# Two of the four weight sums of each seven-product group on GpSimd instead of VectorE

## The chip, the cores and the metric
One core of a Trainium2 chip runs the kernel; the other seven are not used. The metric is the device time of one execution in microseconds (us), the median of three runs.

## The reference
One decoder layer on x of 256 tokens by 2048 channels, all float32. Every stage starts with an RMSNorm:
```python
x = x + 0.5 * swiglu(rmsnorm(x, ffn1_norm), w_gate, w_up, w_down)     # 2048 -> 5632 -> 2048
h = rmsnorm(x, mix_norm)
proj = h @ w_in                                                       # q, k, v of two mixers, gates
y_dil, y_fox = dilated_attention(...), forgetting_attention(...)      # 8 heads of 128 each
merged = sigmoid(g_d + b) * (y_dil @ w_proj_dil) + sigmoid(g_f + b) * (y_fox @ w_proj_fox)
x = x + merged @ w_out
x = x + 0.5 * swiglu(rmsnorm(x, ffn2_norm), w_gate2, w_up2, w_down2)
return rmsnorm(x, final_norm)
def swiglu(x, w_gate, w_up, w_down): return (silu(x @ w_gate) * (x @ w_up)) @ w_down
```
The change touches only the two feed-forward stages (`swiglu`).

## The kernel before
**Precision.** Every float32 weight `w` is used as two parts of the rounded type: ScalarE copies it into `w_hi`, VectorE computes `w_lo = w - w_hi`, and the same is done for activations. A product is three matmuls (hi hi, hi lo, lo hi), so each weight passes through ScalarE and VectorE once before TensorE may use it.

**Slabs and the ring.** The unit is a slab, two 128-row blocks of 512 columns (128 partitions x 1024 elements). SyncE loads weights in pieces of two slabs (1 MB) into the four buffers `raw`. In the feed-forward stages the split slabs live in a ring of six (`FFN_RING`): `w_hi`/`w_lo` for four of them, `more_hi`/`more_lo` for two. ScalarE may round slab n when TensorE has finished slab n - 6 (semaphore `slab_done`), VectorE splits it after that (`hi_ready`), TensorE waits for the split (`lo_ready`), and SyncE reuses a buffer of `raw` by the count of `lo_ready` in the table `FREE` (lines 84, 424): loads 4 and 5 of a step, the gate and up rows of group 1, go out when the slabs before 5 and before 7 are split; loads 0 and 1 of the coming step when those before -6 and before -4 are.

**A feed-forward step.** The hidden width of 5632 is worked through in eleven chunks of 512. The first is done plainly (`FIRST`, 16 slabs), the ten others are the steps of a loop (`STEPS`, 30 slabs each), and there are two such stages, `ffn(0)` and `ffn(1)`, with the mixers between them: 20 steps in all. A step has, in this order (`step_slab`, line 88): seven slabs of group 0, four plain slabs 7 to 10, seven slabs 11 to 17 of group 1, four plain slabs 18 to 21, and eight slabs 22 to 29 of the down projection for the chunk before. A plain or down slab takes 12 matmuls, a group's slab 6.

**A group** computes gate and up for both token halves from seven products instead of eight, in the manner of Strassen and Winograd. Four of the seven weight operands are sums of blocks of the raw gate weights G and up weights U (even and odd rows of blocks):
```python
PRODUCTS = (("sum", T3), ("sum", T1), ("gate", 1), ("sum", T4), ("gate", 0), ("sum", T2), ("up", 1))
# T3 = U[odd] - U[even]   T1 = U[even] - G[even]   T2 = T3 + G[even]   T4 = G[odd] - T2
```
They lie in `sums`, one set of four 128x1024 tiles for both groups, and count as slabs 0, 1, 3 and 5 of their group. ScalarE rounds them like any slab (`round_step`, line 912, waiting on `summed`), VectorE splits them (`split_step`, line 1191).

**The order of the work** is written out by hand on each engine, each queue is in order, and semaphores alone join the queues. ScalarE and VectorE run six slabs ahead of TensorE in their programs: in the loop's slot o they handle slab o + 6. On VectorE, `early_sums` (line 1181) makes T3 and T1 of group 1 just before the split of slab 10, and those of the next step's group 0 just before the split of slab 29; it first waits for the load. T2 follows the split of the group's first slab and T4 that of its second.

**The hidden chunk.** TensorE transposes the chunk's hidden activations (line 585), the two token halves one after the other in one PSUM bank; ScalarE rounds each half into `hT_hi` (line 959) and VectorE makes `hT_lo` (line 1263). The second half's rounding stands behind the rounding of slab 11 in ScalarE's program (slot o == 5), and its `hT_lo` behind the split of slab 11 and T2 in VectorE's. TensorE waits for it between slabs 8 and 9 (line 657); slab 9 begins with line 694 (`direct_up`). Lines 520 to 522 are the matmuls of plain slabs, 533 to 535 those of a group, 1283 the add of a down result to `xres`.

**GpSimd** has no program in this kernel.

Of the kernel before, what the change touches and what calls it, by code (L numbers as in the profile page):

```python
# [80 lines left out]
PRODUCTS = (("sum", T3), ("sum", T1), ("gate", 1), ("sum", T4), ("gate", 0), ("sum", T2), ("up", 1))  # L81
SUMS = 8 * STEPS

# [88 lines left out]
def build(nc, x, ffn1_norm, ffn1_w_gate, ffn1_w_up, ffn1_w_down, mix_norm, w_in, b_forget,  # L172
# [144 lines left out]
    final_gain_landed = sem("final_gain_landed")  # L317
    stored = sem("stored")
    summed = sem("summed")
    s_ready = sem("s_ready")  # L320
# [74 lines left out]
    block = nc.Block()  # L395
    with block:

        @block.sync
# [494 lines left out]
        def _(act):  # L893
# [18 lines left out]
            def round_step(place, offset, count):  # L912

                q, r = divmod(offset, STEP)
                kind, g, o = step_slab(r)
                src, l = step_source(r)
                if l is None:
                    act.wait_ge(summed, count + 8 * q + 4 * g + (T3, T1, T2, T4).index(PRODUCTS[o][1]) + 1)
                else:
                    act.wait_ge(raw_landed[l % LOADS], place.landed(STEP_LOADS * q + l))  # L920
                act.wait_ge(slab_done, place.slab(offset - FFN_RING + 1))
                nc.scalar.activation(slot_hi(place, offset), src, ACT.Copy).then_inc(hi_ready, 1)  # L922
# [70 lines left out]
            def ffn(f, b):  # L993
# [26 lines left out]
                def step(place, i, last):  # L1020
                    merged = (i + f * STEPS) * COMBINED
                    for o in range(STEP):
                        if not last or o + FFN_RING < STEP:
                            round_step(place, o + FFN_RING, i * 8 + count)
                        else:
# [141 lines left out]
        def _(dve):  # L1167
# [12 lines left out]

            def early_sums(place, q, g):

                gate, up = 0, 1
                dve.wait_ge(raw_landed[up], place.landed(STEP_LOADS * q + 4 * g + up))
                nc.vector.tensor_tensor(sums[:, T3], raw[:, up, 1::2, :], raw[:, up, 0::2, :],
                                        ALU.subtract).then_inc(summed, 1)
                dve.wait_ge(raw_landed[gate], place.landed(STEP_LOADS * q + 4 * g + gate))
                nc.vector.tensor_tensor(sums[:, T1], raw[:, up, 0::2, :], raw[:, gate, 0::2, :],
                                        ALU.subtract).then_inc(summed, 1)

            def split_step(place, offset, count, final=False):

                q, r = divmod(offset, STEP)
                if r in (10, STEP - 1) and not (final and r == STEP - 1):

                    early_sums(place, *((q, 1) if r == 10 else (q + 1, 0)))
                kind, g, o = step_slab(r)
# [3 lines left out]
                if kind == "paired" and o in (0, 1):  # L1201
                    done, gate = count + 8 * q + 4 * g, 0
                    if o == 0:
                        dve.wait_ge(summed, done + 1)
                        nc.vector.tensor_tensor(sums[:, T2], sums[:, T3], raw[:, gate, 0::2, :],
                                                ALU.add).then_inc(summed, 1)
                    else:
                        dve.wait_ge(summed, done + 3)
                        nc.vector.tensor_tensor(sums[:, T4], raw[:, gate, 1::2, :], sums[:, T2],  # L1209
# [106 lines left out]
            def ffn(f, b):  # L1316
                first = first_place(f)
                silu, count = f * FF_CHUNKS * TT, f * SUMS
                for o in range(FIRST):
                    m = o + FFN_RING  # L1320
                    if m < FIRST:
                        if m == FIRST - 1:
                            early_sums(step_place(f), 0, 0)
                        split_slab(first, m)
# [31 lines left out]
                def step(place, i, last):  # L1356
                    hid, merged = i * TT + HID[f], (i + f * STEPS) * COMBINED
                    u3, u2 = partial[:, PART_U3], partial[:, PART_U2]
                    for o in range(STEP):
                        if not last or o + FFN_RING < STEP:  # L1360
                            split_step(place, o + FFN_RING, i * 8 + count, last)
                        else:
# [224 lines left out]
```

## Time and profile before
| what | value |
|---|---|
| median of three runs | 2142.38 us (2140.95 to 2144.67) |
| the profiled execution | 2140.0 us, its span 2138.2 us |
| granted TensorE clock, mean | 0.996 of full |
| busy: TensorE, VectorE, ScalarE, GpSimd | 98%, 75%, 51%, 0% |
| DMA | 402.88 MB, 188 GB/s |

The times of the engines overlap: a share of busy time says how full an engine is, and not what it costs. A VectorE record of 1.22 us is followed by the next 1.14 us later, so the records of a stream overlap a little; the matmul records of 0.39 us follow one another every 0.23 us. "Idle before" names what ended an engine's idle time. PE is TensorE, DVE is VectorE, ACT is ScalarE, POOL is GpSimd, SP is SyncE.

### The profile page before, as it was taken

Reading aid. Unit: us, or ns where it says so; the run is one execution under the profiler, and the core shown is the slowest. Engines: PE = TensorE matmul, PEld = TensorE weight load, DVE = VectorE, ACT = ScalarE, POOL = GpSimd, SP = SyncE. Lnnn points to the kernel's source line nnn. Section 1 sums busy time; section 2 is a strip of 40 time slices with the busy share of each in tenths; the row PEclk is TensorE's granted clock in tenths of the full one; section 3 lists DMA queues with packets and bytes.
Section 4 is the critical chain, followed back from the end, with each engine's and each line's share of the span. In section 5 each row is a group of like instructions: output and inputs, shape, how many; then the busy total and the mean of one; then the engine's idle time right before and its main releaser. Section 6 shows DMA issues by size and latency. Waiting matters only on the chain.

```text
span 2138.2 us, 26519 instructions
## 1 busy us (share of the span) xinstructions
PE 2097.6 (98%) x9475; PEld 1728.2 (81%) x9475; DVE 1606.8 (75%) x1613; ACT 1090.8 (51%) x1259; POOL 0.2 (0%) x4
## 2 busy tenths in 40 slices
PE   7999999999999999999999999999999999999997
PEld 5788888888887888888888888878888888888876
DVE  6888888888888744444455555688888889888886
ACT  5545555545555544555454344465555555555553
POOL 0000000000000000000000000000000000000000
PEclk9999999999999999999999999999999999999999
DMA  7556566556566545545445665555565665555652
GB/s 247 187 167 215 177 217 214 182 171 216 177 216 207 167 158 180 188 160 171 158 164 183 204 206 185 189 190 199 162 204 188 216 206 195 166 201 188 220 198 98
DMA packets 204643, 402.88 MB, mean 188 GB/s; under 512 B 8576, under 2 KB 8752, under 8 KB 204464
## 3 DMA queue, kind: packets, MB, share of 16 engines
q1 hardware_dynamic: 202032, 401.64, 56.1%
q10 hardware_dynamic: 2560, 0.55, 0.1%
q8 instruction: 34, 0.56, 0.1%
q14 instruction: 17, 0.14, 0.0%
HBM read 400.06 MB, written 2.10 MB: 188 GB/s over the span
## 4 chain that ended last, share of the span: by engine, by line
PE 93%; DVE 3%; ACT 2%; DMA 1%; issue 1%; SPq 0%; ACTq 0%; DVEq 0%
PE ps L520 21%; PE ps L522 21%; PE ps L521 21%; PE ps L533 6%; PE ps L535 6%; PE ps L534 6%; PE ps L694 3%; PE ps L696 3%; PE ps L695 3%; PE ps L585 1%; DMA raw<-in_ffn_w_gate 1%; DMA raw<-in_ffn_w_up 1%; DVE xres L1283 1%; DVE w_lo L1178 1%; ACT chunk_buf L946 0%
## 5 line engine op out<-in xcount | busy, mean ns | idle before, releaser
L1178 DVE TENSOR_TENSOR w_lo<-raw,w_hi 128x1024 fp32r<-128x1024 f32 x256 | 312.6, 1224 | 312.2 <-ACT w_hi L909 311.9
L909 ACT ACTIVATE w_hi<-raw 128x1024 fp32r<-128x1024 f32 x256 | 269.8, 1059 | 313.0 <-PE ps L522 307.1
L922 ACT ACTIVATE w_hi<-raw 128x1024 fp32r<-128x1024 f32 x300 | 317.8, 1059 | 218.0 <-PE ps L522 97.6
L1199 DVE TENSOR_TENSOR w_lo<-raw,w_hi 128x1024 fp32r<-128x1024 f32 x300 | 366.4, 1221 | 77.3 <-ACT w_hi L922 66.5
L520 PE MATMUL ps<-w_hi,xT_hi 128*128 128x512 f32 x816 | 321.6, 394 | 7.1 <-DVE w_lo L1178 6.7
L522 PE MATMUL ps<-w_hi,xT_lo 128*128 128x512 f32 x816 | 318.6, 390 | 0.0
L521 PE MATMUL ps<-w_lo,xT_hi 128*128 128x512 f32 x816 | 318.3, 390 | 0.0
L520 PE MATMUL ps<-w_hi,hT_hi 128*128 128x512 f32 x576 | 224.4, 390 | 0.0
L522 PE MATMUL ps<-w_hi,hT_lo 128*128 128x512 f32 x576 | 224.1, 389 | 0.0
L521 PE MATMUL ps<-w_lo,hT_hi 128*128 128x512 f32 x576 | 224.1, 389 | 0.0
L922 ACT ACTIVATE w_hi<-sums 128x1024 fp32r<-128x1024 f32 x100 | 106.2, 1062 | 223.0 <-DVE sums L1209 111.8
L922 ACT ACTIVATE more_hi<-raw 128x1024 fp32r<-128x1024 f32 x140 | 148.6, 1062 | 103.0 <-PE ps L522 70.8
L1199 DVE TENSOR_TENSOR more_lo<-raw,more_hi 128x1024 fp32r<-128x1024 f32 x140 | 169.4, 1221 | 39.7 <-ACT more_hi L922 34.3
L520 PEld LDWEIGHTS ps<-w_hi,xT_hi 128*128 128x128 f32 x816 | 153.8, 189 | 38.7 <-issue 7.2
L522 PEld LDWEIGHTS ps<-w_hi,xT_lo 128*128 128x128 f32 x816 | 153.6, 188 | 32.5
L521 PEld LDWEIGHTS ps<-w_lo,xT_hi 128*128 128x128 f32 x816 | 153.9, 189 | 30.7
L1199 DVE TENSOR_TENSOR w_lo<-sums,w_hi 128x1024 fp32r<-128x1024 f32 x100 | 122.2, 1222 | 37.6 <-ACT w_hi L922 36.3
L1283 DVE SCALAR_TENSOR_TENSOR xres<-ps,xres 128x1024 f32<-128x1024 f32 x104 | 126.4, 1216 | 6.2 <-PE ps L522 6.2
L694 PE MATMUL ps<-w_hi,xT_hi 128*128 128x512 f32 x320 | 125.2, 391 | 1.9 <-DVE hT_lo L1263 1.9
L522 PEld LDWEIGHTS ps<-w_hi,hT_lo 128*128 128x128 f32 x576 | 108.1, 188 | 22.5
L521 PEld LDWEIGHTS ps<-w_lo,hT_hi 128*128 128x128 f32 x576 | 108.2, 188 | 22.4
L520 PEld LDWEIGHTS ps<-w_hi,hT_hi 128*128 128x128 f32 x576 | 108.1, 188 | 22.3
(212 smaller groups left out, 3635.6 us busy)
## 6 DMA issues: line engine op xcount, KB each, us to landing
raw<-in_ffn_w_gate SPq DMA_DIRECT2D x88, 1024.0 KB, 5.1
raw<-in_ffn_w_up SPq DMA_DIRECT2D x88, 1024.0 KB, 5.2
raw<-in_ffn_w_down SPq DMA_DIRECT2D x88, 1024.0 KB, 5.1
raw<-in_w_in SPq DMA_DIRECT2D x80, 1024.0 KB, 5.0
raw<-in_w_out SPq DMA_DIRECT2D x16, 1024.0 KB, 5.0
raw<-in_w_proj_dil SPq DMA_DIRECT2D x8, 1024.0 KB, 5.0
raw<-in_w_proj_fox SPq DMA_DIRECT2D x8, 1024.0 KB, 4.9
xres<-in_x SPq DMA_DIRECT2D x4, 512.0 KB, 7.1
```

The lines of the kernel that those rows point to most:

```text
L520: nc.tensor.matmul(acc, hi, hi_w[:, j], start=first and j == 0, stop=False)
L521: nc.tensor.matmul(acc, hi, lo_w[:, j], start=False, stop=False)
L522: done = nc.tensor.matmul(acc, lo, hi_w[:, j], start=False, stop=last and j == 1)
L533: nc.tensor.matmul(acc, hi, hi_w[:, j], start=first and j == 0, stop=False)
L534: nc.tensor.matmul(acc, hi, lo_w[:, j], start=False, stop=False)
L535: done = nc.tensor.matmul(acc, lo, hi_w[:, j], start=False, stop=last and j == 1)
L694: nc.tensor.matmul(acc, hi, hi_w[:, j], start=begin, stop=False)
L909: nc.scalar.activation(slot_hi(place, offset), raw_half(place, offset), ACT.Copy).then_inc(hi_ready, 1)
L922: nc.scalar.activation(slot_hi(place, offset), src, ACT.Copy).then_inc(hi_ready, 1)
L1178: nc.vector.tensor_tensor(slot_lo(place, offset), raw_half(place, offset), slot_hi(place, offset).bitcast(F32), ALU.subtract).then_inc(lo_ ...
L1199: nc.vector.tensor_tensor(slot_lo(place, offset), step_source(r)[0], slot_hi(place, offset).bitcast(F32), ALU.subtract).then_inc(lo_ready, 1)
L1283: nc.vector.scalar_tensor_tensor(xres[:, :, chunk(n)], ps[:, banks:banks + TT], factor, xres[:, :, chunk(n)], ALU.mult, ALU.add)\
```

## The change
T3 and T1 are made by a program of GpSimd's own: for both feed-forward stages a loop over the ten steps, in it both groups. It waits until the slabs before slab -6 (group 0) or before slab 6 (group 1) are split, then for the up load, makes T3, waits for the gate load, makes T1. These two count on a new semaphore `early_summed`; T2 and T4 stay on VectorE and count on `summed`, and their waits and ScalarE's are counted anew. The semaphores' order and the data are the same otherwise.
```diff
--- before.py
+++ after.py
@@ -79,7 +79,7 @@
 PAIR_SLABS = 7
 
 PRODUCTS = (("sum", T3), ("sum", T1), ("gate", 1), ("sum", T4), ("gate", 0), ("sum", T2), ("up", 1))
-SUMS = 8 * STEPS
+SUMS = 4 * STEPS
 
 FREE = (-6, -4, -2, 0, 5, 7, 9, 11, 16, 18, 20, 22)
 GROUP_ORDER = (1, 0, 3, 2)
@@ -316,6 +316,7 @@
     gate_bias_landed = sem("gate_bias_landed")
     final_gain_landed = sem("final_gain_landed")
     stored = sem("stored")
+    early_summed = sem("early_summed")
     summed = sem("summed")
     s_ready = sem("s_ready")
     s_hi = sem("s_hi")
@@ -395,6 +396,24 @@
     block = nc.Block()
     with block:
 
+        @block.gpsimd
+        def _(pool):
+            gate, up = 0, 1
+            for f in range(2):
+                with pool.Fori(0, STEPS) as i:
+                    place = step_place(f, i)
+                    for g in range(2):
+                        if g == 0:
+                            pool.wait_ge(lo_ready, place.slab(-6))
+                        else:
+                            pool.wait_ge(lo_ready, place.slab(6))
+                        pool.wait_ge(raw_landed[up], place.landed(4 * g + up))
+                        nc.gpsimd.tensor_tensor(sums[:, T3], raw[:, up, 1::2, :], raw[:, up, 0::2, :],
+                                                ALU.subtract).then_inc(early_summed, 1)
+                        pool.wait_ge(raw_landed[gate], place.landed(4 * g + gate))
+                        nc.gpsimd.tensor_tensor(sums[:, T1], raw[:, up, 0::2, :], raw[:, gate, 0::2, :],
+                                                ALU.subtract).then_inc(early_summed, 1)
+
         @block.sync
         def _(sp):
             sp.dma_start(gain_rows[0:KT, :], ffn1_norm.rearrange("l (k p) -> (l k) p", p=P))\
@@ -915,7 +934,8 @@
                 kind, g, o = step_slab(r)
                 src, l = step_source(r)
                 if l is None:
-                    act.wait_ge(summed, count + 8 * q + 4 * g + (T3, T1, T2, T4).index(PRODUCTS[o][1]) + 1)
+                    made = early_summed if PRODUCTS[o][1] in (T3, T1) else summed
+                    act.wait_ge(made, count + 4 * q + 2 * g + (T3, T1, T2, T4).index(PRODUCTS[o][1]) % 2 + 1)
                 else:
                     act.wait_ge(raw_landed[l % LOADS], place.landed(STEP_LOADS * q + l))
                 act.wait_ge(slab_done, place.slab(offset - FFN_RING + 1))
@@ -1021,7 +1041,7 @@
                     merged = (i + f * STEPS) * COMBINED
                     for o in range(STEP):
                         if not last or o + FFN_RING < STEP:
-                            round_step(place, o + FFN_RING, i * 8 + count)
+                            round_step(place, o + FFN_RING, i * 4 + count)
                         else:
                             round_slab(last_place(f), o + FFN_RING - STEP)
                         if o == 2:
@@ -1178,34 +1198,21 @@
                 nc.vector.tensor_tensor(slot_lo(place, offset), raw_half(place, offset),
                                         slot_hi(place, offset).bitcast(F32), ALU.subtract).then_inc(lo_ready, 1)
 
-            def early_sums(place, q, g):
-
-                gate, up = 0, 1
-                dve.wait_ge(raw_landed[up], place.landed(STEP_LOADS * q + 4 * g + up))
-                nc.vector.tensor_tensor(sums[:, T3], raw[:, up, 1::2, :], raw[:, up, 0::2, :],
-                                        ALU.subtract).then_inc(summed, 1)
-                dve.wait_ge(raw_landed[gate], place.landed(STEP_LOADS * q + 4 * g + gate))
-                nc.vector.tensor_tensor(sums[:, T1], raw[:, up, 0::2, :], raw[:, gate, 0::2, :],
-                                        ALU.subtract).then_inc(summed, 1)
-
             def split_step(place, offset, count, final=False):
 
                 q, r = divmod(offset, STEP)
-                if r in (10, STEP - 1) and not (final and r == STEP - 1):
-
-                    early_sums(place, *((q, 1) if r == 10 else (q + 1, 0)))
                 kind, g, o = step_slab(r)
                 dve.wait_ge(hi_ready, place.slab(offset + 1))
                 nc.vector.tensor_tensor(slot_lo(place, offset), step_source(r)[0],
                                         slot_hi(place, offset).bitcast(F32), ALU.subtract).then_inc(lo_ready, 1)
                 if kind == "paired" and o in (0, 1):
-                    done, gate = count + 8 * q + 4 * g, 0
+                    done, gate = count + 4 * q + 2 * g, 0
                     if o == 0:
-                        dve.wait_ge(summed, done + 1)
+                        dve.wait_ge(early_summed, done + 1)
                         nc.vector.tensor_tensor(sums[:, T2], sums[:, T3], raw[:, gate, 0::2, :],
                                                 ALU.add).then_inc(summed, 1)
                     else:
-                        dve.wait_ge(summed, done + 3)
+                        dve.wait_ge(summed, done + 1)
                         nc.vector.tensor_tensor(sums[:, T4], raw[:, gate, 1::2, :], sums[:, T2],
                                                 ALU.subtract).then_inc(summed, 1)
 
@@ -1319,8 +1326,6 @@
                 for o in range(FIRST):
                     m = o + FFN_RING
                     if m < FIRST:
-                        if m == FIRST - 1:
-                            early_sums(step_place(f), 0, 0)
                         split_slab(first, m)
                     else:
                         split_step(step_place(f), m - FIRST, count)
@@ -1358,7 +1363,7 @@
                     u3, u2 = partial[:, PART_U3], partial[:, PART_U2]
                     for o in range(STEP):
                         if not last or o + FFN_RING < STEP:
-                            split_step(place, o + FFN_RING, i * 8 + count, last)
+                            split_step(place, o + FFN_RING, i * 4 + count, last)
                         else:
                             split_slab(last_place(f), o + FFN_RING - STEP)
                         if o == 2:
```

## Rows read from the trace of the kernel before
**Rows 1.** The page, part 1: busy us, share of the span, instructions, by engine.
```profile
PE 2097.6 (98%) x9475; PEld 1728.2 (81%) x9475; DVE 1606.8 (75%) x1613; ACT 1090.8 (51%) x1259; POOL 0.2 (0%) x4
```

**Rows 2.** Waits of TensorE: engine and line, released by; us in total, times, longest.
```profile
PE ps L520 <- DVE w_lo L1178: 6.7, 2, 4.1
...
PE ps L694 <- DVE hT_lo L1263: 1.9, 2, 1.1
```

**Rows 3.** VectorE timeline, third step: start us, us, line, operation, tiles, idle before.
```profile
208.94 1.21 DVE L1199 TENSOR_TENSOR w_lo<-raw,w_hi 128x1024 fp32r<-128x1024 f32 x1
210.74 1.23 DVE L1185 TENSOR_TENSOR sums<-raw 128x1024 f32<-128x1024 f32 x1 [0.59 <-DMA raw<-in_ffn_w_up]
211.89 1.22 DVE L1188 TENSOR_TENSOR sums<-raw 128x1024 f32<-128x1024 f32 x1
213.02 1.22 DVE L1199 TENSOR_TENSOR w_lo<-raw,w_hi 128x1024 fp32r<-128x1024 f32 x1
214.16 1.22 DVE L1199 TENSOR_TENSOR w_lo<-sums,w_hi 128x1024 fp32r<-128x1024 f32 x1
215.29 1.22 DVE L1205 TENSOR_TENSOR sums<-sums,raw 128x1024 f32<-128x1024 f32 x1
216.43 0.68 DVE L1263 TENSOR_TENSOR hT_lo<-ps,hT_hi 128x512 fp32r<-128x512 f32 x1
```

**Rows 4.** Timeline of TensorE in the same step.
```profile
217.05 0.39 PE L522 MATMUL ps<-w_hi,xT_lo 128*128 128x512 f32 x1
217.27 0.47 PE L694 MATMUL ps<-w_hi,xT_hi 128*128 128x512 f32 x1
```

**Rows 5.** Timelines, VectorE and TensorE: first step, last of `ffn(0)`.
```profile
86.91 0.68 DVE L1263 TENSOR_TENSOR hT_lo<-ps,hT_hi 128x512 fp32r<-128x512 f32 x1
...
88.78 0.39 PE L694 MATMUL ps<-w_hi,xT_hi 128*128 128x512 f32 x1
...
667.82 0.68 DVE L1263 TENSOR_TENSOR hT_lo<-ps,hT_hi 128x512 fp32r<-128x512 f32 x1
...
668.56 0.50 PE L694 MATMUL ps<-w_hi,xT_hi 128*128 128x512 f32 x1 [1.15 <-DVE hT_lo L1263]
```

**Rows 6.** Timeline of VectorE where the third and the fourth step begin.
```profile
204.21 2.35 DVE L1199 TENSOR_TENSOR more_lo<-raw,more_hi 128x1024 fp32r<-128x1024 f32 x2
...
266.27 1.22 DVE L1199 TENSOR_TENSOR w_lo<-sums,w_hi 128x1024 fp32r<-128x1024 f32 x1 [0.38 <-ACT w_hi L922]
```

**Rows 7.** Waits of VectorE.
```profile
DVE sums L1185 <- DMA raw<-in_ffn_w_up: 12.1, 19, 2.0
```

**Rows 8.** Groups of VectorE instructions: count, busy us, mean ns, idle before.
```profile
L1185 DVE TENSOR_TENSOR sums<-raw 128x1024 f32<-128x1024 f32 x40 | 48.8, 1220 | 12.1 <-DMA raw<-in_ffn_w_up 12.1
L1188 DVE TENSOR_TENSOR sums<-raw 128x1024 f32<-128x1024 f32 x40 | 48.7, 1218 | 0.0
```

**Rows 9.** Timeline of VectorE, end of the third step.
```profile
251.06 1.22 DVE L1185 TENSOR_TENSOR sums<-raw 128x1024 f32<-128x1024 f32 x1
...
255.60 1.21 DVE L1199 TENSOR_TENSOR more_lo<-sums,more_hi 128x1024 fp32r<-128x1024 f32 x1
```

**Rows 10.** Timeline of ScalarE, third step.
```profile
208.82 1.06 ACT L922 ACTIVATE w_hi<-raw 128x1024 fp32r<-128x1024 f32 x1 [0.23 <-PE ps L535]
...
212.08 1.06 ACT L922 ACTIVATE w_hi<-sums 128x1024 fp32r<-128x1024 f32 x1 [2.20 <-DVE sums L1185]
...
213.05 0.57 ACT L959 ACTIVATE hT_hi<-ps 128x512 fp32r<-128x512 f32 x1
```

**Rows 11.** Timeline of SyncE: when loads are issued.
```profile
214.27 0.37 SPq L425 DMA_DIRECT2D raw<-in_ffn_w_up  x1
...
240.32 0.37 SPq L425 DMA_DIRECT2D raw<-in_ffn_w_up  x1
```

**Rows 12.** The page, part 6: DMA issues, KB each, median us to landing.
```profile
raw<-in_ffn_w_up SPq DMA_DIRECT2D x88, 1024.0 KB, 5.2
```

**Rows 13.** Busy time in one step's stretch, by engine (instructions), TensorE clock, DMA share.
```profile
201.00:265.30 64.30, 64.11 (x284) 52.47 (x284) 56.38 (x52) 34.04 (x36) 0.00 (x0) 1.00 0.58 196
```

## The prediction
> **What bounds the kernel now.** I read the page first, then the waits of TensorE, then one feed-forward step instruction by instruction. TensorE is busy for 98% of the span and VectorE for 75%, while GpSimd does nothing [rows 1]. So time can only be won where TensorE stands idle, and is lost wherever it is made to. Its waits are few: 6.7 us for splits of the plain stages, and 1.9 us, in two of the twenty steps, in front of line 694 [rows 2]. None of its waits in the feed-forward steps is for `sums` or for a slab made from them. By throughput the four sums of a group cost VectorE nothing that TensorE feels.
>
> By latency it is another matter. TensorE may not begin slab 9 of a step (line 694) before the second half of `hT_lo` is written (line 657). Follow VectorE in one step [rows 3]: it splits slab 9, stands idle until the `up` load of group 1 lands, at T = 210.74, and then does in program order T3, T1, the split of slab 10, the split of slab 11 (whose rounding needs T3), T2, and only then `hT_lo`, which starts at 216.43 and takes 0.68: written at 217.11, 6.37 us after T. TensorE streams without a gap and starts line 694 at 217.27 [rows 4]. The slack is 0.16 us. I read the same pair in all 20 steps: it is 1.19 us in the first (87.59 to 88.78), 0.13 to 0.40 in seventeen others, and in the last step of each feed-forward TensorE waits, 1.15 and 0.72 us [rows 5]. The twenty slacks add up to 5.9 us; the hand-over from `hT_lo` to line 694 takes 0.06 (668.50 to 668.56), which leaves about 4.7 us to use up in all.
>
> T itself does not move with the change. The `up` load is issued when slab 6 is split (204.21 plus 1.14), and that split comes behind slab 5's and an add to `xres`; where the next step begins, the split of slab 5 starts at 266.27 after 0.38 us of waiting for ScalarE [rows 6], so VectorE has by then worked off its backlog, and the pace is TensorE's. VectorE waits for this load in 19 of 20 steps, 12.1 us in sum [rows 7].
>
> **The change, part by part.**
> *Removed from VectorE:* 40 T3 and 40 T1, 1.22 us each in the records, 1.14 from start to start [rows 3, 8]: 80 x 1.14 = 91 us. Half are done at the step's end, where VectorE is behind (the T3 at 251.06 and the T1 after it) and has caught up by 266.27 [rows 6, 9]; TensorE does not wait there, so 46 us are worth nothing. The other half stand in the chain T to `hT_lo`, where 2.28 us per step leave.
>
> *Added to the chain:* the same two sums on GpSimd, and two hand-overs. No record of before shows a GpSimd sum. From below its price is VectorE's, 1.14 us; from above three passes over 1024 elements, two operands in and one out, one after the other, at ScalarE's 1.06 us for a one-operand pass [rows 10], 3.2 us. I take two such passes (an engine that fetches its operands in turn and writes beside that), 2.12, and 0.11 for the hand-over from T3's end to the rounding (211.97 to 212.08) [rows 3, 10]: P = 2.23 us. By the Trainium skill, GPSIMD Engine Reference, Reconciling with measured numbers, 2048 float32 elements take GpSimd 4497 ns and VectorE 2293; half of the former is 2.25 us, by which the sum below would be about 1 us larger. This trace shows VectorE's 1.22 for 1024 and no GpSimd sum.
>
> *Whether the two engines stand in each other's way* is the second unknown. From below nothing; from above each waits for a whole instruction of the other, since all of VectorE's splits, like GpSimd's sums, read two operands from SBUF. I take the upper end. In the chain that has two places:
> - Split 10 no longer queues behind the sums. Its rounding ends at 209.88 [rows 10] and split 9 at 210.08, so it runs 210.08 to 211.22, over the landing: T3 starts at T + 0.5.
> - T1 follows T3 at once on GpSimd, as the `gate` half has landed long before. The rounding of slab 11 takes 1.06 after T3, less than P, so split 11 always finds T1 running and waits for its end: T + 0.5 + 2P.
>
> Then split 11, T2 and `hT_lo` follow as before, 2.95 us (214.16 to 217.11) [rows 3]. Sum: T + 0.5 + 4.46 + 2.95 = T + 7.91 against T + 6.37, **1.54 us late per step**. Twenty steps give 31 us, less the 4.7 us of slack: +26 us. Nothing is hidden here, because line 694 is next on TensorE's in-order queue; what is late next, the split of slab 12 and T4, is not needed before TensorE has done slabs 9 and 10 (5.4 us) and slab 11.
>
> The rule behind this choice is in the Trainium skill, SBUF — State Buffer, Who interferes with whom: a VectorE instruction with two SBUF inputs and a GpSimd instruction that reads SBUF share a read interface, and the later one blocks fully until the other ends. Nothing in this trace can show it. By it the sum is the +26 above, without it the first rival's.
>
> *GpSimd at the step's end (group 0):* T3 and T1 can run from the landing of load 1 (issued at 240.32, 5.2 us to landing: near 245.5) [rows 11, 12] to about 250. At worst they hold up one or two splits by up to 2.2 us each, while VectorE saves 2.28 us and still finishes slab 0's split some 10 us before TensorE needs it (split at 255.60, used from 265.3 on) [rows 9, 13]. Cost nothing; if that cover were gone, up to 2 us per step.
> *Waits and queues:* GpSimd's new waits stall nobody else, its queue holds only these sums. Its wait for slab 6 (group 1) is over before the `up` load is even issued. SyncE's loads: the one that waits for split 10 is issued some 3 us earlier (at 214.27 now) [rows 11], and nobody waited for it. VectorE's own wait for T3 before T2 is over when split 11 is done. ScalarE's rounding of slab 11 now hangs on GpSimd, with the second `hT_hi` behind it (0.57 us) [rows 10], inside the time above. The sums in slot order are otherwise the same data, no DMA is added, and two loops on GpSimd run beside all else.
>
> The profiled execution took 2140.0 us (span 2138.2) and the median of the runs is 2142.4; 2142.4 + 26 = **2168 us**. A measurement of this kernel can tell about 0.2%, 4.3 us, from no change.
>
> **The rivals.**
> *No interference.* Then T3 starts at T, and the chain is P + 1.06 for the rounding + 0.1 + 2.95 = T + 6.34, as late as before. T1 runs beside the split. TensorE feels nothing, at best the two waits of 1.9 us shrink: 2140 to 2144 us. For it: the chain has two sums less on VectorE, and 98% of TensorE leaves no more to win. Against it: it needs P under about 2.5 us too (6.37 + 0.29 slack). Above that point every further 0.1 us costs 2 us. 17%.
> *A GpSimd sum near the upper end, 2.8 to 3.2 us.* With interference the lateness is 0.5 + 6.4 + 2.95 - 6.37 = 3.5 us per step, 70 - 5 = +65: 2207 us; at 2.8, +49, 2191. Without it, about 1.0 per step, +15: 2158. 17%.
> *A sum near VectorE's own price, 1.14 to 1.5 us.* With interference 0.5 + 2.28 + 2.95 is T + 5.7, earlier than now: the two waits vanish, 2140.5 us; decisive is P under 1.7. I know no reason for such a pace. 3%.
> *The change doesn't do what it says:* GpSimd's loop is held up by its waits or by its own loop instructions, so that T3 comes 1 us or more after the landing even without interference. Each 1 us costs 20 us: 2158 to 2170. The waits above speak against it; 3%.
>
> **How the numbers follow.** The forecast has a chance of 60%, with P between 1.9 and 2.6: lateness 0.9 to 2.3 us per step, 2155 to 2184 on its own. The range goes down to the first rival's and up into the second's: 2140 to 2192; outside are the upper part of the long sums and little else. Faster by over 0.2% would need 4.3 us, more than the two waits hold: 2%. Within 0.2%: 17 + 3 and the few forecasts that all but fit the slack, less the 2: 20%. Slower: 78%.
>
> **What the changed profile would show.** If right: 80 GpSimd sums, about 2.2 us each; TensorE waiting for `hT_lo` in front of line 694 in 18 or more steps, some 1.3 us each and about 28 us in sum; VectorE's split 11 starting only when T1 ends (or its record longer by that wait), and T3 starting after split 10 rather than at the landing; every step about 65.6 us where it is 64.3 [rows 13]. VectorE's busy time falls by some 97 us, unless waiting counts as busy. Wrong if: split 11 starts 0.1 us after its rounding while T1 runs (no interference), sums of another length, or TensorE waiting for a slab (`w_lo`) at lines 520 or 533 instead, which would put the damage in the ring.

## The result and the profile after

The changed kernel took 2170.35 us (median of 4 runs, 2169.03 to 2172.27) against 2142.64 us before (4 runs of the same session): ratio 1.013, 95% interval 1.0112 to 1.0147. It is 27.7 us slower; the forecast was 2168, a loss of 26.

The page of the changed kernel, parts 1 and 5 (groups: line, engine, operation, tiles, count, then busy us and mean ns, then idle before); line 713 is what line 694 was [rows 1, 8]:

```profile
PE 2097.3 (97%) x9475; PEld 1729.4 (80%) x9475; DVE 1567.2 (72%) x1533; ACT 1091.0 (50%) x1259; POOL 221.9 (10%) x84
...
L411 POOL TENSOR_TENSOR sums<-raw 128x1024 f32<-128x1024 f32 x40 | 107.3, 2684 | 1860.4 <-DMA raw<-in_ffn_w_up 1860.4
L1206 DVE TENSOR_TENSOR w_lo<-sums,w_hi 128x1024 fp32r<-128x1024 f32 x100 | 142.9, 1429 | 120.2 <-ACT w_hi L942 118.9
...
L713 PE MATMUL ps<-w_hi,xT_hi 128*128 128x512 f32 x320 | 126.9, 396 | 28.0 <-DVE hT_lo L1270 28.0
```

TensorE does the same work (2097 us) in a span of 2168.9 instead of 2138.2 us, so all of the loss is idle time. GpSimd is now busy for 222 us: in the records its sums take 2.68 us (T3) and 2.90 us (T1) on the mean. VectorE lost 80 instructions of 1.22 us, 98 us, but its busy time fell by 40 only, from 1606.8 to 1567.2; the splits of `sums`, 1.22 us on the mean before, read 1.43. So waiting does count as busy in these records, the case that the prediction left open.

The waits of TensorE in the changed kernel (us in total, times, longest); the second line of [rows 2] answers to the first:

```profile
PE ps L713 <- DVE hT_lo L1270: 28.0, 20, 1.4
PE ps L552 <- DVE xres L1290: 7.4, 16, 0.5
```

1.9 us in two steps have become 28.0 us in all twenty, 1.4 us each. The 7.4 us for `xres` in front of line 552, the third product of a step, are new as well, and need a second look (below: they cost nothing).

GpSimd in the changed kernel's third step, group 1 and then group 0 of the next step:

```profile
212.59 2.79 POOL L411 TENSOR_TENSOR sums<-raw 128x1024 f32<-128x1024 f32 x1 [23.73 <-DMA raw<-in_ffn_w_up]
215.34 2.40 POOL L414 TENSOR_TENSOR sums<-raw 128x1024 f32<-128x1024 f32 x1
249.08 2.40 POOL L411 TENSOR_TENSOR sums<-raw 128x1024 f32<-128x1024 f32 x1 [31.34 <-DMA raw<-in_ffn_w_up]
251.44 3.39 POOL L414 TENSOR_TENSOR sums<-raw 128x1024 f32<-128x1024 f32 x1
```

VectorE in the same step, for [rows 3]:

```profile
210.79 2.35 DVE L1206 TENSOR_TENSOR w_lo<-raw,w_hi 128x1024 fp32r<-128x1024 f32 x2
216.59 2.24 DVE L1206 TENSOR_TENSOR w_lo<-sums,w_hi 128x1024 fp32r<-128x1024 f32 x1 [3.45 <-ACT w_hi L942]
218.75 1.21 DVE L1212 TENSOR_TENSOR sums<-sums,raw 128x1024 f32<-128x1024 f32 x1
219.89 0.68 DVE L1270 TENSOR_TENSOR hT_lo<-ps,hT_hi 128x512 fp32r<-128x512 f32 x1
```

Read the two together. The first VectorE row is two splits, slabs 9 and 10, and ends at 213.14. The load has landed at 212.59, where GpSimd's T3 begins in the record; it lasts 2.79 us, where an undisturbed sum lasts 2.40 (the rows at 215.34 and 249.08), so it really ran from 212.98, when the split of slab 10 was all but through. T1 follows at 215.34 and ends at 217.74. The split of slab 11 is due at 216.59 and lasts 2.24 us instead of 1.22: it began in truth at 217.6, at the end of T1. T2 and `hT_lo` follow as they did, `hT_lo` is written at 220.57, and line 713 starts at 220.69 [rows 4]. The other steps confirm the reading: T3's record starts 5.99 to 6.44 us after the step's third product, as the load lands, but ends 9.11 to 9.17 us after it in all twenty.

A table of three stretches, from TensorE's starts, shows where in a step the time lies (mean us per step; A: third product to slab 9, B: slab 9 to slab 20, where the second `direct_up` pair begins, both over twenty steps; C: slab 20 to the next step's third product, over the eighteen steps that another one follows):

| kernel | A | B | C | sum |
|---|---|---|---|---|
| before | 13.07 | 20.45 | 30.98 | 64.50 |
| changed | 14.43 | 20.53 | 30.98 | 65.94 |
| e1_group0 | 12.86 | 20.41 | 30.98 | 64.25 |
| e2_group1 | 14.56 | 20.67 | 30.98 | 66.21 |
| e3_t1_late | 13.46 | 20.53 | 31.22 | 65.21 |
| e4_no_meeting | 13.10 | 20.47 | 31.24 | 64.81 |
| e5_before_swap | 12.98 | 20.42 | 30.75 | 64.15 |
| e6_group0_swap | 12.93 | 20.41 | 30.28 | 63.62 |
| e7_after_swap | 14.48 | 20.53 | 30.28 | 65.29 |
| e8_spare_read | 14.81 | 21.18 | 30.98 | 66.97 |
| e9_spare_write | 13.00 | 20.44 | 30.98 | 64.42 |
| e10_earlier_sums | 12.86 | 20.41 | 30.28 | 63.55 |

Twenty times 1.36 (A) and 0.08 (B) are 29 of the 30.7 us by which the span grew.

Three steps of the kernel before are not like the others. In the last step of each stage the `up` load landed 7.7 and 7.3 us after the third product instead of 6.2. In its very first, A is 14.48 instead of 12.88, because TensorE had a lower granted clock there (us; busy and instructions of TensorE, its loads, VectorE, ScalarE, GpSimd; granted clock; DMA share, GB/s):

```profile
74.30:78.00 3.70, 3.70 (x9) 2.99 (x10) 2.04 (x2) 0.74 (x1) 0.00 (x0) 0.54 0.40 92
```

The profiles of e3, e4, e5 and e6 have the same stretch in that step; the changed kernel's and the others do not. Differences in A of less than 0.1 us between kernels say nothing for that reason. In the seventeen ordinary steps A grew by 1.56 and B by 0.09 us.

Times and ratios below are medians against runs of the kernel before on the same chip, there 2138.9 to 2140.7 us.

### The profile page after: what moved, and what is told of

It is laid out like the page before. It is cut to its first block, busy times and chain, and to the rows that moved or that the text cites. A ratio compares the mean times of both kernels' runs of the same rounds, so it can differ in the third digit from the quotient of the medians.

```text
span 2168.9 us, 26517 instructions
## 1 busy us (share of the span) xinstructions
PE 2097.3 (97%) x9475; PEld 1729.4 (80%) x9475; DVE 1567.2 (72%) x1533; ACT 1091.0 (50%) x1259; POOL 221.9 (10%) x84
## 4 chain that ended last, share of the span: by engine, by line
PE 78%; issue 10%; DVE 5%; ACT 3%; POOL 3%; DMA 1%; SPq 0%; ACTq 0%; DVEq 0%; POOLq 0%
PE ps L539 19%; PE ps L541 19%; PE ps L540 19%; PE ps L713 4%; PE ps L715 3%; PE ps L714 3%; PE ps L554 3%; PE ps L553 3%; PE ps L552 3%; POOL sums L411 3%; ACT w_hi L942 2%; DVE w_lo L1206 1%; DVE sums L1212 1%; DMA raw<-in_ffn_w_gate 1%; DVE hT_lo L1270 1%
## 5 line engine op out<-in xcount | busy, mean ns | idle before, releaser
L1198 DVE TENSOR_TENSOR w_lo<-raw,w_hi 128x1024 fp32r<-128x1024 f32 x256 | 316.9, 1242 | 313.0 <-ACT w_hi L928 312.7
L1206 DVE TENSOR_TENSOR w_lo<-raw,w_hi 128x1024 fp32r<-128x1024 f32 x300 | 376.1, 1259 | 75.3 <-ACT w_hi L942 64.5
L411 POOL TENSOR_TENSOR sums<-raw 128x1024 f32<-128x1024 f32 x40 | 107.3, 2684 | 1860.4 <-DMA raw<-in_ffn_w_up 1860.4
L1206 DVE TENSOR_TENSOR w_lo<-sums,w_hi 128x1024 fp32r<-128x1024 f32 x100 | 142.9, 1429 | 120.2 <-ACT w_hi L942 118.9
```

The lines of the kernel that those rows point to most:

```text
L411: nc.gpsimd.tensor_tensor(sums[:, T3], raw[:, up, 1::2, :], raw[:, up, 0::2, :], ALU.subtract).then_inc(early_summed, 1)
L1198: nc.vector.tensor_tensor(slot_lo(place, offset), raw_half(place, offset), slot_hi(place, offset).bitcast(F32), ALU.subtract).then_inc(lo_ ...
L1206: nc.vector.tensor_tensor(slot_lo(place, offset), step_source(r)[0], slot_hi(place, offset).bitcast(F32), ALU.subtract).then_inc(lo_ready, 1)
```

## The experiments

### Which group does the harm: e1_group0 and e2_group1
GpSimd's loop keeps one group; `early_sums` comes back on VectorE for the other, at its old place. The diff is e1_group0's; e2_group1 has `(1,)`, and the call for group 0 before the split of slab 29 as in the kernel before.
```diff
-                    for g in range(2):
+                    for g in (0,):
...
+                if r == 10:
+                    early_sums(place, q, 1)
```


> Only group 0's T3 and T1 on GpSimd, group 1's back on VectorE at its old place. Theory A (the damage is group 1's chain from the landing of the up load to hT_lo, through the length of the sums and the two engines waiting for each other): the chain is the one of before, 6.37 us after the landing, so the wait for hT_lo falls back to about 2 us in sum and the time to 2140 to 2145 us, although two VectorE records at each step's end stay longer. Rival B (any GpSimd sum slows the kernel, by blocking VectorE wherever it runs): half the sums, half the loss, about 2156 us.

Measured 2136.97 us, ratio 0.999 (0.9981 to 1.000); before took 2139.25 on this chip, so the time lies below the range expected and the ratio does not.

> Only group 1's T3 and T1 on GpSimd, group 0's back on VectorE. Theory A: all of the loss stays, 2168 to 2172 us, with 28 us of waiting for hT_lo. The wait of 7.4 us for xres at the head of the step, new in the changed kernel, goes, and the gap of 0.2 us without a named releaser in front of slab 0 comes back, with no change in the time, since the third product starts 30.98 us after the second plain group in both. Rival B: about 2156 us.

Measured 2175.75 us, ratio 1.0162 (1.0146 to 1.0179), above the changed kernel's 1.013. Waits of TensorE in e2_group1:

```profile
PE ps L713 <- DVE hT_lo L1283: 30.8, 20, 3.3
...
PE ps L552 <- issue: 4.4, 18, 0.3
```

All of the loss is group 1's. In e1_group0 the two GpSimd sums of a step take 2.5 and 3.3 us in the records, and VectorE's records next to them are longer, yet A, B and C are those of before or less: rival B fell. It won 2 us (the interval reaches 1.000), as much as the two waits for `hT_lo` in the last steps, which are gone; the rest of its lower A is the first step. e2_group1 lies 4 us above what was expected in three of its four runs (2175.8 us; the fourth took 2170.96), and its profiled execution has it in one place, the first step of the second stage (A 16.30, B 23.18, where nearly all its other steps have 14.4 and 20.5). There the `up` load took 7.6 us to land instead of 5.1, TensorE waited 3.3 us for `hT_lo`, and its granted clock was 0.50 over the 3.7 us behind the wait. Why the load was late is not shown. As expected, the wait for `xres` is gone and the gap is back, at the same C.

### Take the meetings away: e3_t1_late and e4_no_meeting
```diff
                         pool.wait_ge(raw_landed[gate], place.landed(4 * g + gate))
+                        if g == 1:
+                            pool.wait_ge(ht_lo, i * TT + (HID[f] + TT))
```
e4_no_meeting has this too, and in `split_step`:
```diff
+                if r == 10:
+                    dve.wait_ge(early_summed, count + 4 * q + 3)
```


> The changed kernel, in which GpSimd starts group 1's T1 only when the second half of hT_lo is written. Theory A: T1 no longer stands in the way of the split of slab 11 (1.0 us per step), so hT_lo comes at the landing + 0.4 + 2.4 + 1.2 + 2.95 = 6.95 us, 0.3 to 0.6 us late: line 713 waits 0.4 us instead of 1.4 in each step and the time is 2148 to 2153 us, faster although a wait is added. T1 of slab 12 comes 3.7 us later but is hidden under slabs 9 and 10. Rival C (the engines do not wait for each other; the whole loss is that a GpSimd sum takes 2.4 to 2.8 us instead of 1.2): the time stays at 2170 us or rises.

Measured 2155.48 us, ratio 1.0076 (1.0059 to 1.0093): above the 2148 to 2153 expected.

> As e3_t1_late, and VectorE splits slab 10 only after T3 of group 1 is made, so that neither of the two sums of group 1 meets a VectorE instruction. Theory A: T3's record falls from 2.8 to 2.4 us and starts at the landing; the split of slab 10 runs beside ScalarE's rounding of slab 11. hT_lo at the landing + 2.4 + 1.2 + 2.95 = 6.55 us, within the slack of 0.3 us: 2141 to 2147 us, so the mere length of the sums costs next to nothing. Rival C: still 15 us or more above before.

Measured 2143.26 us, ratio 1.0018 (1.0008 to 1.0027). GpSimd in e4_no_meeting, then VectorE:

```profile
210.62 2.39 POOL L411 TENSOR_TENSOR sums<-raw 128x1024 f32<-128x1024 f32 x1 [23.46 <-DMA raw<-in_ffn_w_up]
217.30 2.39 POOL L416 TENSOR_TENSOR sums<-raw 128x1024 f32<-128x1024 f32 x1 [4.30 <-DVE hT_lo L1274]
```
```profile
208.88 1.22 DVE L1210 TENSOR_TENSOR w_lo<-raw,w_hi 128x1024 fp32r<-128x1024 f32 x1
213.13 1.23 DVE L1210 TENSOR_TENSOR w_lo<-raw,w_hi 128x1024 fp32r<-128x1024 f32 x1 [3.03 <-POOL sums L411]
214.27 1.22 DVE L1210 TENSOR_TENSOR w_lo<-sums,w_hi 128x1024 fp32r<-128x1024 f32 x1
215.41 1.22 DVE L1216 TENSOR_TENSOR sums<-sums,raw 128x1024 f32<-128x1024 f32 x1
216.54 0.68 DVE L1274 TENSOR_TENSOR hT_lo<-ps,hT_hi 128x512 fp32r<-128x512 f32 x1
```

Two added waits take the ratio from 1.013 to 1.0018, 24 us. T3 lasts 2.39 us from the landing on; the split of slab 10 waits for it and is done beside ScalarE's rounding; the split of slab 11 lasts 1.22 us. `hT_lo` is written at 217.22, 6.60 us after the landing, and A is 13.10, as before. So sums of twice the length leave the chain 0.2 us longer than before and all but fit the slack, and rival C, that the length alone did it, fell. By A, T1 against the split of slab 11 cost 0.97 us per step (e3), T3 against the split of slab 10 0.36 (e4); in ordinary steps, without the first and those around the stages' ends, it is 1.02 and 0.55.

That a later T1 would be hidden was wrong for both. C grew by 0.25 us per step. In e3_t1_late the down loads go out later and closer together, group 0's `up` load lands 6.75 us after its issue (242.09 to 248.84) where it took 5.3 (243.77 to 249.08 in the changed kernel), and GpSimd's group 0 T3 (248.84 to 251.25) then starts just ahead of the split of slab 28 and holds it up for nearly its whole length. VectorE, then TensorE:

```profile
249.00 3.33 DVE L1208 TENSOR_TENSOR w_lo<-raw,w_hi 128x1024 fp32r<-128x1024 f32 x1 [1.49 <-ACT w_hi L944]
...
265.94 1.21 DVE L1292 SCALAR_TENSOR_TENSOR xres<-ps,xres 128x1024 f32<-128x1024 f32 x1
```
```profile
267.76 0.49 PE L554 MATMUL ps<-more_hi,pair_hi 128*128 128x512 f32 x1 [0.85 <-DVE xres L1292]
```

The first row is that split, 3.33 us instead of 1.22; the second is the third add to `xres`, which is late by it, and for which TensorE then waits in front of the next step's slab 0. It waits for an add to `xres` for 9.7 us in 13 steps, in nine of them for this third one, in the others for the fourth. This is the remainder to before in e4 as well (10.4 us in 14 steps).

### The dispute by itself: e8_spare_read and e9_spare_write
The kernel before, with a GpSimd loop whose result nobody uses (what it writes, `gate_buf`, is free in these steps; ScalarE waits for `spare_done` before it uses it).
```diff
+                with pool.Fori(0, STEPS - 1) as i:
+                    place = step_place(f, i)
+                    pool.wait_ge(spare_done, i * 1 + (1 + f * (STEPS - 1) * 1))
+                    pool.wait_ge(raw_landed[up], place.landed(4 + up))
+                    nc.gpsimd.tensor_tensor(gate_buf[:, 0]..., xT_hi[:, 0:4].bitcast(F32),
+                                            xT_lo[:, 0:4].bitcast(F32), ALU.subtract)
```
e9_spare_write subtracts one column instead and then does a `memset` of `gate_buf`, 2047 columns.

> The kernel before, all four sums on VectorE, and beside it one GpSimd subtraction of the same size per step (18 of the 20 steps), started at the landing of group 1's up load, that reads parts of xT_hi and xT_lo and writes a buffer nobody reads. No instruction of the layer waits for it in those steps. Theory A (a GpSimd instruction that reads SBUF and a VectorE instruction with two SBUF inputs exclude each other): one VectorE record in the chain grows by up to 2.4 us, hT_lo comes 0.3 to 2.1 us late, and the time is 5 to 38 us above before, most likely about 2160 to 2175 us. Rival C (only the length of the sums mattered): no VectorE record grows and the time is that of before.

Measured 2191.59 us, ratio 1.0251 (1.0227 to 1.0275). Timelines of e8_spare_read, GpSimd and VectorE:

```profile
213.44 3.45 POOL L408 TENSOR_TENSOR gate_buf<-xT_hi,xT_lo 128x1024 f32<-128x1024 f32 x1 [63.03 <-DMA raw<-in_ffn_w_up]
```
```profile
213.40 1.22 DVE L1201 TENSOR_TENSOR sums<-raw 128x1024 f32<-128x1024 f32 x1 [0.52 <-DMA raw<-in_ffn_w_up]
214.54 3.43 DVE L1204 TENSOR_TENSOR sums<-raw 128x1024 f32<-128x1024 f32 x1
217.89 1.22 DVE L1215 TENSOR_TENSOR w_lo<-raw,w_hi 128x1024 fp32r<-128x1024 f32 x1
```

This is the cleanest picture of the mechanism. VectorE's T3 starts first, at 213.40, and keeps its 1.22 us. GpSimd's instruction, released at 213.44, lasts 3.45: about 1.05 of waiting and 2.40 of work, until 216.89. VectorE's T1, due at 214.54, lasts 3.43: it stands still until GpSimd is done. No instruction of these steps depends on GpSimd's result, and the kernel is 51 us slower. More than was expected: 35 us are in A, and 15 us in B, by a second effect that the last section shows.

> As e8_spare_read, but GpSimd subtracts one column only and then fills 2047 columns with a constant, so that it is busy for 1 to 3 us at the same place and reads next to nothing. Theory A with the shared read side alone: no VectorE record grows by more than 0.1 us and the time is within 3 us of before. Rival F (any GpSimd instruction that touches SBUF blocks VectorE): as e8_spare_read.

Measured 2140.58 us, ratio 1.000 (0.9991 to 1.001). Timelines of e9_spare_write, GpSimd and VectorE:

```profile
209.19 1.23 POOL L408 TENSOR_TENSOR gate_buf<-xT_hi,xT_lo 128x1 f32<-128x1 f32 x1 [61.29 <-DMA raw<-in_ffn_w_up]
210.35 1.81 POOL L410 MEMSET gate_buf<- 128x2047 f32 x1
```
```profile
209.14 1.23 DVE L1202 TENSOR_TENSOR sums<-raw 128x1024 f32<-128x1024 f32 x1 [0.46 <-DMA raw<-in_ffn_w_up]
210.28 1.22 DVE L1205 TENSOR_TENSOR sums<-raw 128x1024 f32<-128x1024 f32 x1
211.42 1.22 DVE L1216 TENSOR_TENSOR w_lo<-raw,w_hi 128x1024 fp32r<-128x1024 f32 x1
```

GpSimd is busy from 209.19 to 212.16, and its `memset`, 1.81 us of that, lies across two VectorE instructions, T1 and the split behind it, that keep their 1.22 us. So a GpSimd instruction that only writes SBUF excludes nothing here, and rival F fell; that the `memset` is also another kind of instruction than a subtraction is not separated by this run. The trace agrees with the rule of the Trainium skill, SBUF — State Buffer, Who interferes with whom, by which a VectorE instruction with two SBUF inputs contends with a GpSimd instruction that reads SBUF and not with one that only writes it.

### The head of the step: e5_before_swap, e6_group0_swap, e7_after_swap, e10_earlier_sums
Why did the new wait of 7.4 us for `xres` cost nothing, C being 30.98 in both kernels? TensorE at the fourth step's head, before:

```profile
264.75 0.39 PE L522 MATMUL ps<-w_hi,hT_lo 128*128 128x512 f32 x1
265.36 0.49 PE L533 MATMUL ps<-more_hi,pair_hi 128*128 128x512 f32 x1 [0.22 <-issue]
...
268.76 0.49 PE L533 MATMUL ps<-w_hi,xT_hi 128*128 128x512 f32 x1
```

and in the changed kernel:

```profile
268.20 0.39 PE L541 MATMUL ps<-w_hi,hT_lo 128*128 128x512 f32 x1
268.42 0.39 PE L552 MATMUL ps<-more_hi,pair_hi 128*128 128x512 f32 x1
...
272.20 0.49 PE L552 MATMUL ps<-w_hi,xT_hi 128*128 128x512 f32 x1 [0.46 <-DVE xres L1290]
```

Before, slab 0 starts 0.61 us after the last matmul of the step, where the pace is 0.23; after, it starts at the pace, and the third product waits for `xres` instead. From the last matmul to the third product it is 4.01 and 4.00 us. In the program there are two candidates: the loop ends with a wait for the third add to `xres`, which VectorE in its backlog has only then, and the third product waits for the fourth add, which stands behind the split of slab 5. VectorE before:

```profile
263.54 1.21 DVE L1283 SCALAR_TENSOR_TENSOR xres<-ps,xres 128x1024 f32<-128x1024 f32 x1
...
267.41 1.22 DVE L1283 SCALAR_TENSOR_TENSOR xres<-ps,xres 128x1024 f32<-128x1024 f32 x1
```

The third add ends at 264.75, when the last matmul starts, and the fourth at 268.63, 0.13 before the third product. The edit, called the swap below, puts that add ahead of the split:
```diff
                     for o in range(STEP):
+                        if o == STEP - 1:
+                            add_down(place, STEP, NN - 1, DOWN_BANKS[NN - 1], 0.5)
                         if not last or o + FFN_RING < STEP:
...
-                        if o > STEP - DOWN and o % 2 == 1:
+                        if STEP - DOWN < o < STEP - 1 and o % 2 == 1:
```


> The kernel before, in which VectorE adds the fourth down result to xres ahead of the split of the next step's slab 5 and not behind it. Theory D (in the kernel before, two limits tie at the head of a step: VectorE's backlog, which releases the third add to xres just too late for the loop's last wait and costs the gap of 0.4 to 0.5 us in front of slab 0, and this fourth add): only one of the two is taken away, so little is won, 0 to 3 us. What may shrink is the chain to hT_lo, since the split of slab 6 comes 0.4 us earlier: 2137 to 2140 us if before stands at 2139. Rival E (the gap in front of slab 0 is the loop's own cost and nothing is tied to it): the same 0 to 3 us, so this run speaks only together with e6_group0_swap.

Measured 2133.45 us, ratio 0.9967 (0.9954 to 0.9979): 7 us where 0 to 3 were expected. The gap in front of slab 0 is there still (3.5 us in 16 steps), but C fell by 0.23 us: the fourth add had been the later of the two by that much. The waits of the last steps for `hT_lo` fell from 1.9 to 0.6 us (A by 0.09).

> e1_group0 (only group 0's T3 and T1 on GpSimd) with the same swap as e5_before_swap. Theory D: GpSimd's sums take away the backlog and with it the gap in front of slab 0, the swap takes away the wait of 7.4 us for xres, and the third product can start 0.46 us earlier in each of 16 steps or more: 7 to 9 us less than e1_group0, about 2129 us. Rival E: the gap comes back in another place and the time stays at 2136 us.

Measured 2125.77 us, ratio 0.9928 (0.9911 to 0.9945). C is 30.28, 0.70 less than before, where GpSimd's group 0 sums alone gave nothing and the swap alone 0.23. That is 11 us below e1_group0, where 7 to 9 were expected, and the gap did not come back in another place: rival E fell. Two limits that tie must both go.

> The changed kernel with the swap of e5 and e6 (the fourth add to xres ahead of the split of slab 5). Theory D: the wait for xres (7.4 us) goes, and because the split of slab 6, the issue and the landing of group 1's up load move 0.4 us ahead against TensorE, the wait for hT_lo shrinks by about 0.4 us per step as well: 2170 - 7 - 8 = about 2155 us. If only the wait for xres were removed: 2163 us.

Measured 2158.55 us, ratio 1.0095 (1.0078 to 1.0112). C fell by 0.70, but A not at all. The landing moved ahead, and T3 did not: GpSimd in e7_after_swap:

```profile
210.83 3.10 POOL L411 TENSOR_TENSOR sums<-raw 128x1024 f32<-128x1024 f32 x1 [22.72 <-DMA raw<-in_ffn_w_up]
213.90 2.40 POOL L414 TENSOR_TENSOR sums<-raw 128x1024 f32<-128x1024 f32 x1
```

T3's record starts 6.0 us after the third product (204.82), where in the changed kernel it was 6.3, but ends after 9.11 us in both (213.93 here; 215.38 after 206.27). What lets T3 in is the end of the split of slab 10, which hangs on TensorE's pace, and not the landing: the expectation that A would gain 0.4 us was wrong, and this is why. T3's record ends 9.11 to 9.18 us after the third product in nineteen steps of this kernel; in the one left the load itself landed late.

e10_earlier_sums has the swap on the kernel before, no GpSimd, and
```diff
-                if r in (10, STEP - 1) and not (final and r == STEP - 1):
+                if r in (10, STEP - 2) and not (final and r == STEP - 2):
```


> The kernel before with the swap, no GpSimd: VectorE makes group 0's T3 and T1 one slab earlier (ahead of the split of slab 28 of the step before and not 29), in the 2.7 us in which it otherwise idles there. Theory D (what GpSimd's group 0 sums are worth is only that VectorE is through its backlog sooner): most of the gap in front of slab 0 goes without GpSimd, 2126 to 2131 us if before stands at 2140. Rival: only GpSimd's help removes the backlog, and the time stays at that of e5_before_swap, 0.997 of before.

Measured 2124.72 us, ratio 0.9936 (0.992 to 0.9953), the same as e6_group0_swap within the intervals. VectorE in e10_earlier_sums:

```profile
242.52 1.22 DVE L1185 TENSOR_TENSOR sums<-raw 128x1024 f32<-128x1024 f32 x1
243.65 1.22 DVE L1188 TENSOR_TENSOR sums<-raw 128x1024 f32<-128x1024 f32 x1
244.79 1.22 DVE L1199 TENSOR_TENSOR w_lo<-raw,w_hi 128x1024 fp32r<-128x1024 f32 x1
...
258.84 1.22 DVE L1283 SCALAR_TENSOR_TENSOR xres<-ps,xres 128x1024 f32<-128x1024 f32 x1
...
262.04 1.22 DVE L1283 SCALAR_TENSOR_TENSOR xres<-ps,xres 128x1024 f32<-128x1024 f32 x1 [0.40 <-PE ps L522]
```

T3 and T1 of group 0 fill a stretch in which VectorE idled, the third add is done at 260.06, 4.9 us before the third product (264.92) where it was 4.0, and the fourth waits for TensorE alone. All that GpSimd did for this kernel VectorE does by itself, with the sums one slab earlier and the swap. Against the kernel before it wins 14 us, where the changed kernel loses 28.

## Why the prediction was right

**The place** was right: the loss is the wait for `hT_lo` in front of slab 9, 28.0 us of waiting against about 28 named, in 20 steps of 1.4 us against "18 or more, some 1.3 us each", and a step takes 65.9 us against 65.6. No wait for a slab of the ring appeared, and e1 and e2 put it all in group 1.

**The chain**, term by term: T + 0.5 for the split of slab 10 was 0.4 in the third step and 0.48 on the mean of all. P, taken as 2.23 with 0.11 for a hand-over in it, was too small: a sum takes 2.40 in the record, and 2.35 from start to start where two undisturbed ones follow each other (e2_group1, first step of the second stage). `hT_lo` came 7.98 us after T in the third step (212.59 to 220.57) and 7.88 to 8.31 in all, 8.07 on the mean of the ordinary ones, against 7.91. The estimate of 2.25 us by the Trainium skill, GPSIMD Engine Reference, Reconciling with measured numbers, is the length of a sum without a hand-over. The rows' figure to set beside it is 2.12, and the measured 2.40 is above both.

**The choice** between no interference and whole-instruction exclusion, which nothing in the trace of before could decide, was the step on which all hung; e8 shows exclusion directly, e9 that a GpSimd `memset` is free of it, and e4 about what the first rival would have given: a ratio of 1.0018, which is 2146.5 us where before takes 2142.6, just above its 2140 to 2144, and the excess is in C, where the sums of group 0 still meet VectorE. The rival of a GpSimd sum near 3 us looks right in the records (2.68 and 2.90 on the mean), but they hold the waiting; the undisturbed rows say 2.40.

**Luck in the number.** The forecast loss was made of 1.3 us in each ordinary step and 3.5 us in the three others. Measured by A and B it was 1.65 us in each of seventeen ordinary steps, 28.0 us, and 0.9 in the three others. The ordinary steps lost more because `hT_lo` came 1.70 us later and not 1.54, because the hand-over to line 713 takes 0.13 us there and not 0.06, and by the 0.09 in B. The three others lost less: the slack of 1.19 us in the first step stood behind TensorE's lower clock and was not there in the changed kernel, and the last steps' late landings, which the prediction took as given, did not come again. The first error is 6 us, the second 3 us the other way, so the number came out closer than its terms.

**What was missed:** "TensorE does not wait there, so 46 us are worth nothing" held in time and not in its reason. TensorE did lose 0.70 us per step at the step's head to VectorE's backlog (C 30.98 against 30.28 in e6 and e10), 0.4 to 0.5 of it in a gap without a named releaser; that gap stayed worth nothing because the fourth add to `xres` tied with it. And a stop costs TensorE a little beyond its length: the matmul after it is followed 0.1 us late, the 0.08 us in B. Against the forecast 26 us, all of them in A, stand 27 in A and 2 in B.

## What to carry to other kernels
Moving work off a busy engine helps only if that engine's throughput is what is waited for; here it was the latency of one chain, with 0.1 to 0.4 us of slack in most steps, and what its links lose beyond that is lost in every step. GpSimd arithmetic that reads SBUF is not parallel to VectorE instructions with two SBUF operands: count both engines' instructions as one queue wherever they meet, and place GpSimd's where VectorE idles or takes one operand from PSUM. A new wait that costs nothing points at a tie: look for the older limit under it, since removing both may pay.

## What was not expected of the hardware
**A short stop can cost more than itself.** In e8_spare_read, eight of twenty steps have B at 22.1 to 22.2 us instead of 20.5. Stretches of that kernel behind two waits for `hT_lo`, one in which it happened and one in which it didn't (columns: us; busy and instructions of TensorE, its loads, VectorE, ScalarE, GpSimd; granted clock; DMA share, GB/s):

```profile
207.15:220.16 13.01, 13.01 (x59) 10.44 (x58) 11.86 (x9) 7.82 (x9) 3.45 (x1) 1.00 0.63 215
222.11:225.80 3.69, 3.69 (x9) 2.90 (x10) 3.62 (x4) 1.06 (x1) 0.00 (x0) 0.54 0.42 163
225.80:244.22 18.42, 18.42 (x82) 15.23 (x82) 13.93 (x13) 10.99 (x11) 0.00 (x0) 1.00 0.71 247
289.97:293.60 3.63, 3.63 (x16) 3.00 (x17) 3.56 (x4) 1.38 (x2) 0.00 (x0) 1.00 0.42 164
```

TensorE ran at the full clock up to 220.16, waited 1.95 us, and then got a granted clock of 0.54 for 3.7 us, most of it at the lower level, 1.2 GHz: nine matmuls instead of sixteen. It cost 1.6 us in the step, and eight times that is 13 of the 15 us in B, the restarts being the rest. In the other steps, after waits of 1.5 to 1.99 us, the clock stayed at full, and it fell behind none of the changed kernel's 20 waits of 1.4 us. It is not GpSimd's doing: the kernel before has it too, in its first step (0.54 over 3.70 us, above), behind a wait of 1.89 us, and e2_group1 behind its wait of 3.3 us. Which waits it strikes is left open.

**What is held up, and what is not.** In the changed kernel GpSimd's T1 of group 0 (251.44, 3.39 us) meets two other kinds of VectorE instruction:

```profile
252.48 1.21 DVE L1395 TENSOR_TENSOR up_sums<-ps,up_sums 128x1024 f32<-128x1024 f32 x1
253.83 1.55 DVE L1284 SCALAR_TENSOR_TENSOR hidden<-up_sums,rstd,chunk_buf 128x512 f32<-128x512 f32 x1
```

The first, with one of its two tensors in PSUM, lies wholly within T1's record and keeps its 1.21 us, as it does in all 18 such steps; T1 itself, held up by the split before (250.68 to 252.56), works from about 252.4 on, its end less 2.40. The second, a `scalar_tensor_tensor` with its tensors in SBUF, is held up like the splits: this first of the two in a step reads 1.54 to 1.56 us in 18 steps, where it is 0.75 in the kernel before, and the mean of all rose from 747 to 1105 ns.

**A one-column read may wait as well.** The 128x1 subtraction in e9_spare_write took 1.23 us in all 18 steps, and ended (210.42) when VectorE's T3 did (210.37). But both start at the same landing in every step, so a fixed length of 1.2 us would look the same, and no run tells the two apart.
